# The values' chunk first in the second block, and loads released slot by slot

## The reference

```python
x = first_block(x, ...)    # mixer, then PEER: every token gathers 128 expert rows
x = second_block(x, ...)   # forgetting + band attention, layer norm, conv FFN, layer norm

# end of the first block: 8 heads x 16 experts a token, u and v rows of 1024 each
a = gelu(einsum('cd,chkd->chk', x_c, u_tab[e_c]))
x = x + gate2 * einsum('chk,chkd->cd', g_c * a, v_tab[e_c])
x = rmsnorm(x, norm_final_g)

# start of the second block
proj = x @ w_in            # q_a, k_a, v_a (512 columns each), forget gate (8), q_b, k_b, v_b
log_f = log_sigmoid(f_a + b_forget)
y_a = forgetting_attention(q_a, k_a, v_a, log_f)       # causal, decay from cumsum(log_f)
y_b = chunked_band_attention(q_b, k_b, v_b, rel_bias)
x = layer_norm(ALPHA * x + concat(y_a, y_b) @ w_out, ...)
```

## Time and profile before

| | |
|---|---|
| median of 3 runs | 1195.69 us |
| profiled execution | 1200.46 us, its span 1198.6 us |
| TensorE matmul busy | 1067.8 us, 89% |
| VectorE, ScalarE, GpSimd busy | 822.1, 427.7, 287.2 us |
| transfers | 389.39 MB, mean 325 GB/s |
| gathers (GpSimd's queue) | 268.45 MB, 54.2% of 16 engines' span |
| all other loads (SyncE's queue) | 120.07 MB, 25.6% |
| chain that ended last | TensorE 52%, DMA 30%, VectorE 12% |

### The profile page before, as it was taken

How to read it: one execution, slowest core, us unless ns; L and a number is a source line. 1 busy time by engine, 2 the same in 40 slices (tenths; PEclk the granted TensorE clock), 3 DMA queues, 4 the chain that set the end, 5 groups by cost and what they waited for, 6 DMA issues and landing times.

```text
span 1198.6 us, 13458 instructions
## 1 busy us (share of the span) xinstructions
PE 1067.8 (89%) x4938; PEld 711.9 (59%) x4938; DVE 822.1 (69%) x1893; ACT 427.7 (36%) x895; POOL 287.2 (24%) x260
## 2 busy tenths in 40 slices
PE   5998999999999987887877888778799999999997
PEld 3797986754444442332332333323399879999986
DVE  5697675757677677778887455555565677888843
ACT  3535631413332232222222111111365664656631
POOL 0000000345354442453544454444000000000000
PEclk8998999999999998888989899998889998999999
DMA  9984593999999999999999999999683342654530
GB/s 374 426 332 183 243 398 151 393 379 421 422 421 422 420 423 420 421 422 420 420 421 422 421 422 422 421 422 421 260 338 141 141 176 81 236 190 167 207 141 36
DMA packets 47878, 389.39 MB, mean 325 GB/s; under 512 B 5442, under 2 KB 5826, under 8 KB 7236
## 3 DMA queue, kind: packets, MB, share of 16 engines
q0 software_dynamic: 36864, 268.45, 54.2%
q1 hardware_dynamic: 10948, 120.07, 25.6%
HBM read 387.45 MB, written 1.05 MB: 324 GB/s over the span
## 4 chain that ended last, share of the span: by engine, by line
PE 52%; DMA 30%; DVE 12%; ACT 3%; issue 1%; POOL 1%; SPq 1%; DVEq 0%; POOLq 0%
DMA ring<-in_uv,idx 24%; PE ps L1783 17%; PE ps L1423 16%; PE ps L1909 5%; DMA ring<-in_w_ada 5%; DVE ring L1237 4%; PE ps L1634 2%; PE ps L1839 2%; PE ps L1445 2%; DMA ring<-in_w_in 2%; DVE ring L887 2%; PE ps L1581 1%; PE ps L1651 1%; DVE ring_r L876 1%; ACT L731 1%
## 5 line engine op out<-in xcount | busy, mean ns | idle before, releaser
L1783 PE MATMUL ps<-ring,probT 128*128 128x512 f32 x1020 | 500.6, 638 | 96.9 <-ACT probT L736 96.7
L1237 DVE CUSTOM_DVE_ANT_0 ring<-h2t,ring 128x1024 f32<-128x1024 f32 x255 | 308.8, 1223 | 169.1 <-DMA ring<-in_uv,idx 168.7
L1783 PEld LDWEIGHTS ps<-ring,probT 128*128 128x128 f32 x1020 | 201.4, 203 | 346.3 <-issue 205.8
L488 POOL DMA_INDIRECT ring<-in_uv,idx x255 | 286.0, 1121 | 346.0 <-PE ps L1783 288.8
L1423 PE MATMUL ps<-util_r,ring_r 128*128 128x256 f32 x1312 | 219.3, 285 | 0.5 <-DVE util_r L1209 0.5
L1423 PEld LDWEIGHTS ps<-util_r,ring_r 128*128 128x128 f32 x1312 | 183.9, 192 | 2.0 <-issue 1.9
L876 DVE TENSOR_TENSOR ring_r<-ring,ring_r 128x1024 fp32r<-128x1024 f32 x134 | 157.8, 1221 | 29.4 <-ACT ring_r L504 29.4
L504 ACT ACTIVATE ring_r<-ring 128x1024 fp32r<-128x1024 f32 x134 | 134.0, 1051 | 49.4 <-DMA ring<-in_w_in 25.8
L731 ACT ACTIVATE prob<-prob 128x2 f32<-128x2 f32 (+2 forms) x94 | 19.2, 204 | 367.5 <-DVE prob L1237 367.4
L1423 PE MATMUL ps<-h_r,ring_r 128*128 128x256 f32 x704 | 125.3, 281 | 0.0
L736 ACT ACTIVATE probT<-ct,prob 128x128 f32<-128x128 f32 x256 | 85.1, 392 | 73.8 <-DVE prob L1243 73.8
(11 more groups left out here) (214 smaller groups left out, 985.4 us busy)
## 6 DMA issues: line engine op xcount, KB each, us to landing
ring<-in_w_in SPq DMA_DIRECT2D x13, 2048.0 KB, 12.5
ring<-in_w_up SPq DMA_DIRECT2D x11, 2048.0 KB, 7.9
ring<-in_w_ada SPq DMA_DIRECT2D x7, 2048.0 KB, 9.8
ring<-in_w_down SPq DMA_DIRECT2D x6, 2048.0 KB, 7.9
ring<-in_w_ada SPq DMA_DIRECT2D x8, 1024.0 KB, 16.3
ring<-in_w_out SPq DMA_DIRECT2D x4, 2048.0 KB, 7.9
ring<-in_w_q SPq DMA_DIRECT2D x3, 2048.0 KB, 9.7
ring<-in_w_br SPq DMA_DIRECT2D x2, 2048.0 KB, 12.7
```

Of the source, the lines that this page charges most:

```text
L488: e.indirect_dma_start(out=row_buf[n], out_offset=None, in_=uv, in_offset=bass.IndirectOffsetOnAxis(ap=idx[:, tt, k:k + 1], axis=0)).then_inc(
L1237: e.tensor_tensor_reduce(u, h2t[:, tt, :], u, 1.0, 0.0, ALU.mult, ALU.add, av[:, tt, n % 128:n % 128 + 1]).then_inc(*made.put(("dot", n)))
L1783: ins = e.matmul(acc[half][:, :], diag[:, n % 8, :], row_buf[n][:, D + half * 512:D + (half + 1) * 512], start=(k == 0), stop=(k == 127))
```

## The change

Five edits that belong together.
1. `BATCHES`: steps 232 to 247 share a gelu by two, no longer by four.
2. The first chunk loaded and used in the second block is ("in2", 2), the values'. The first four go 2, 0, 1, 3 into slots 3, 0, 2, 1. Its quarters become Q2 to Q2+3, those of chunks 0 and 1 Q2+4 to Q2+11; `high_place` puts the quarters from Q2 on four places further, so that the first four lie in slot 5 (last step 248) and the next four in slot 4 (last step 255).
3. SyncE's wait for step 255's arrival is gone: each of the first four loads waits for the last step of its slot alone.
4. TensorE multiplies the values' first half for the first tile ahead of the second tile's turning, then the second half for the first tile, then both halves for the second tile, and only then the columns of chunks 0 and 1.
5. ScalarE and VectorE split Q2 and Q2+1 ahead of the last squares and sums, Q2+2 and Q2+3 ahead of the turned tile's split; the values are copied out of PSUM before the forget gate's work, the keys' second copy stands behind the lows of Q2+12 to Q2+15.

```diff
-    then = ([("in2", i) for i in range(6)] + [("out2", 0), ("out2", 1)]
+    then = ([("in2", i) for i in (2, 0, 1, 3, 4, 5)] + [("out2", 0), ("out2", 1)]
-    chunks = first + [(kind, i, slot) for (kind, i), slot in zip(then, [1, 0, 3, 2] * 6 + [1])]
+    chunks = first + [(kind, i, slot) for (kind, i), slot in zip(then, [3, 0, 2, 1] * 6 + [3])]
...
-Q2 = QUARTER["in2", 0, 0]
+Q2 = QUARTER["in2", 2, 0]
+def high_place(q):
+    return (q + (HI // 2 if q >= Q2 else 0)) % HI
-BATCHES = [(n, 2) for n in range(0, 96, 2)] + [(n, 4) for n in range(96, 248, 4)] + [(n, 1) for n in range(248, 256)]
+BATCHES = ([(n, 2) for n in range(0, 96, 2)] + [(n, 4) for n in range(96, 232, 4)] + [(n, 2) for n in range(232, 248, 2)]
+           + [(n, 1) for n in range(248, 256)])
...
-            sp.wait_ge(arrived[255], 255)
...
-                        act.wait_ge(done, ("rows", last_rows[NW + q % HI // 4]))
+                        act.wait_ge(done, ("rows", last_rows[NW + high_place(q) // 4]))
...
+            split_high(Q2, Q2 + 1)
             sqrt_table(45)
             row_squares(3, 1)
             row_root(3, 1)
-            split_high(Q2, Q2 + 1)
+            split_high(Q2 + 2, Q2 + 3)
             for half in range(2):
                 turned_high(3, hi_r, 1, half)
-            split_high(*range(Q2 + 2, Q2 + 8))
+            split_high(*range(Q2 + 4, Q2 + 10))
+            copy_unit(unit("in2", 0, 0), qa[:, 0:2, :], -0.125)
             act.wait_ge(made, "fe")
...
-            for z in (0, 2):
-                copy_unit(unit("in2", 0, z), qa[:, z:z + 2, :], -0.125)
-                split_high(Q2 + 8 + z, Q2 + 9 + z)
+            split_high(Q2 + 10, Q2 + 11)
+            copy_unit(unit("in2", 0, 2), qa[:, 2:4, :], -0.125)
             copy_unit(unit("in2", 1, 0), ka[:, 0:2, :])
             split_high(*range(Q2 + 12, Q2 + 16))
...
+            split_low(Q2, Q2 + 1)
             rows_added(3, 1)
             row_gain(1, 0)
             row_part(3, 1)
             row_gain(1, 1)
             row_diagonal(3, 1)
-            split_low(Q2)
+            split_low(Q2 + 2, Q2 + 3)
             for half in range(2):
                 turned_low(3, hi_r, lo_r, 1, half)
-            split_low(*range(Q2 + 1, Q2 + 4))
             x3_again(1)
             split_low(*range(Q2 + 4, Q2 + 8))
+            for tt in range(2):
+                dve.wait_ge(done, ("tokens", 2, tt))
+                e.tensor_copy(va[:, tt, :], bank(("tokens", 2, tt))[:, :]).then_inc(*made.put(("v", 2, tt)))
+            split_low(Q2 + 8, Q2 + 9)
...
-            split_low(*range(Q2 + 8, Q2 + 12))
+            split_low(Q2 + 10, Q2 + 11)
+            split_low(*range(Q2 + 12, Q2 + 16))
             copy_unit(unit("in2", 1, 2), ka[:, 2:4, :])
-            split_low(*range(Q2 + 12, Q2 + 16))
-            for tt in range(2):
-                dve.wait_ge(done, ("tokens", 2, tt))
-                e.tensor_copy(va[:, tt, :], bank(("tokens", 2, tt))[:, :]).then_inc(*made.put(("v", 2, tt)))
...
-            turned_x(3, 1)
-
             def both(k):
                 return [("x low", 3, 0, k // 4), ("x low", 3, 1, k // 4)]
 
+            tokens("in2", 2, 0, xs, lambda k: [("x low", 3, 0, k // 4)], (0,))
+            turned_x(3, 1)
+            tokens("in2", 2, 2, xs, lambda k: [], (0,))
+            for z in (0, 2):
+                tokens("in2", 2, z, xs, both, (1,))
             columns("in2", 0, 0, xs, both, acted)
...
             columns("in2", 1, 0, xs, both, acted)
             columns("in2", 1, 2, xs, both, made)
-            tokens("in2", 2, 0, xs, both)
-            tokens("in2", 2, 2, xs, both)
```

More of the change, by code:

```diff
@@ L65 @@
 USED = ("ada", "in", "br", "out", "keys", "q", "in2", "out2", "up", "down")
-QUARTERS = [(kind, i, slot, z) for kind, i, slot, nq in sorted(CHUNKS, key=lambda c: (USED.index(c[0]), c[1])) for z in range(nq)]
+QUARTERS = [(kind, i, slot, z) for kind, i, slot, nq in sorted(
+    CHUNKS, key=lambda c: (USED.index(c[0]), -1 if c[0:2] == ("in2", 2) else c[1])) for z in range(nq)]
 QUARTER = {(kind, i, z): q for q, (kind, i, _, z) in enumerate(QUARTERS)}
 SLOT_OF = {(kind, i): slot for kind, i, slot, _ in CHUNKS}
-Q2 = QUARTER["in2", 0, 0]
+Q2 = QUARTER["in2", 2, 0]
+def high_place(q):
+    return (q + (HI // 2 if q >= Q2 else 0)) % HI
 FIRST_BUFS = ((0, 1), (2, 0), (2, 1), (1, 0), (1, 1), (3, 0), (3, 1))
@@ L273, in quarter @@
             w, lo = part(slots[slot]), part(slots_r[slot])
-            a = NW * SLOT + (q % HI) * 1024
+            a = NW * SLOT + high_place(q) * 1024
             hi = ring_r[:, a:a + w.shape[1] * w.shape[2]].rearrange("p (k n) -> p k n", k=w.shape[1])
@@ L1426, in columns, with tokens @@
                 banks.give(name, freed, emptied or name)
-            def tokens(kind, i, z, x, x_ready):
+            def tokens(kind, i, z, x, x_ready, tiles=range(2)):
                 if z == 0:
-                    group(("tokens", i, 0))
-                    group(("tokens", i, 1))
+                    for tt in tiles:
+                        group(("tokens", i, tt))
                 q = QUARTER[kind, i, z]
-                a = NW * SLOT + (q % HI) * 1024
+                a = NW * SLOT + high_place(q) * 1024
                 wh = ring_r[:, a:a + 2048].rearrange("p (q k n) -> p k q n", q=2, k=KD)
```

## The result

The change made the kernel slower: median 1206.39 us against 1196.01 us, 9 runs each, ratio 1.0072 with a 95% interval of 1.0058 to 1.0087, that is 8.6 us (the two medians differ by 10.4 us; below, times are compared by the ratio and its interval, because the median of before itself moved between 1196.01 and 1199.62 us from one series of runs to the next). The prediction was 1209, slower, in a range of 1195 to 1215.

A forecast was written before the change was run, and what follows sets the result against it. Gathers bound the kernel until about 860 us, TensorE afterwards. With row 255 17.1 us late and gains of 2.35 and 1.6 us, S came 13.1 us later: 1195.7 + 13.1 = 1209 us, range 1195 to 1215.

The forecast's parts named there:

- Part 3: Second-block loads released by each slot's last row: alternating with gathers on the lagging engine, they make row 255 17.1 us late.
- the last dot: Start of the dot product of row 255, the last expert row: forecast at 876.4 us, 859.32 us before.
- the rows' end: Instant when TensorE finishes the expert rows: forecast 880.3 us, or 882.0 at half clock, against 865.55 before.
- S: Instant of the second block's first scores on TensorE, after which all was taken as fixed: forecast 924.5 us, 911.36 before.
- Row 255 is late by 3 x 4.9 + 4 x 0.61 = 17.1 us: On the lagging DMA engine, three whole loads and four packets of the fourth get in before the last row.
- its packets start about 1.3 us later: First early load, issued at 843.4 us: its packets start at 844.7 us, with rows 249 to 255 still queued.
- Part 2: Values' chunk first, behind the last rows: TensorE's waits removed, splits ahead of the row chain added; gain 1.6 us.
- Part 1: Late rows from 232 on in twos: TensorE's backlog goes, rows end at 863.2 us; gain 2.35 us, at worst 0.
- rival C: Other queue shares on the lagging engine: equal bytes 1205.3 us, loads first 1211.3, or 1214.3 with half clock; chance 0.20.
- A: Gathers keep their pace, or loads use only engines done early: S at 907.4, 1191.7 us, faster; chance 0.22.
- B: Loads get one packet per four to eight of the rows: row 255 late by 3.8 to 6.9 us; chance 0.12.
- D: Early release of loads doesn't happen because SyncE is held by another wait: about 1196 us; chance 0.01.

The follow-up runs named there:

- one_early: The changed kernel with only the first load let out behind step 246, the three others waiting for step 255's arrival: 1202.48 us, ratio 1.0039.
- half_early: The changed kernel with half the first chunk, in 8 KB packets, loaded behind step 246; all whole loads wait for step 255's arrival: one run, 1203.41 us.
- late_slots: The kernel before with steps 232 to 247 in twos, no wait for step 255's arrival, first loads into slots 2, 0, 3, 1: 1196.78 us, ratio 0.9991.
- twos: The kernel before with steps 232 to 247 in batches of two, nothing else changed: 1196.54 us, ratio 0.9989.
- nowait: The kernel before with only SyncE's wait for step 255's arrival removed: 1196.81 us, ratio 0.9995.

## Why the prediction was right, and where a size was off

**Part 3, direction and mechanism.** Right: the first load at 843.92 us (forecast 843.4), alternation packet by packet, 4.9 us a load on the path of the rows, no load wait behind the last row. The signs of the forecast came in part: the last dot at 869.34 us and not near 876, the rows' end at 873.48 and not near 881, S at 917.55 and not 925. The term that was mis-sized is "Row 255 is late by 3 x 4.9 + 4 x 0.61 = 17.1 us": it measured 9.8, two whole loads. The step under it that failed is "its packets start about 1.3 us later". With the row queue full the first packet came 3.5 us after the issue (847.4 us; also 3.4 in one_early, and 3.4 in half_early), against 1.0 us with empty queues in before and on the idle engines of late_slots. So row 250 landed untouched, its slot was free early, and the second load's packets stood right behind the first's; between them they held row 252 back by 8.6 us and row 253 by 9.8, which is what the working has for row 253. The term is lost at the third load: its packets were to start at 864.4 us. TensorE, at half clock behind 4.72 us of idle time (granted 0.50 over 862 to 866 us), had read row 252 only by 866.7 us, and the load was issued at 866.72. The idle engines took it up 1.0 us later, at 867.7; the one still busy with row 255 did not disturb it in the 2.6 us left to the last dot. So the third load (4.9 us) and the four packets of the fourth (2.4 us) cost nothing. The delay limits itself: each release waits for a row that the load before has delayed. That later start and later release are the cause is read from these instants; no run changed one of them alone, so how the 7.3 us divide between them is open.

The working also slips by its own rule: from 844.7 us to row 250's landing at 847.0 are seven packets of rows, so one for one the row would have been late by 4.3 us (seven of 0.61), not by 2.5. That lies in the part that the 3.5 us made void.

**Part 2.** S came 44.1 us after the end of the rows, forecast 44.2 (917.55 - 873.48). The gain set against it, 1.6 us, was off: before's 45.8 contains the whole turning at half clock (3.78 us) and a first load released late by the backlog (TensorE waits 0.51 us for the low part); twos, with a turning of 3.38 us and no such wait, has 44.4, so by these traces part 2 brings 0.3 us with weights at hand. The idle time it fills comes back as splits ahead of the row chain (2.4 us) and as the uncovered copy (1.0 us).

**Part 1.** Right in what it does, 2.35 us forecast, about 1.3 us measured (0.1 to 2.6), because the fall to half clock that it guards against is not in every execution. For the same reason the base was wrong: S of 911.36 us stood 3.5 us later than in an execution of the old order without the fall. The base's 3.5 us are 2.1 in the rows' end and 1.4 behind it, just what parts 1 and 2 were credited with removing. The errors had opposite signs: 7.3 us too much delay, 1.3 us too much gain in part 2 and 2.35 in part 1. So 13.1 was forecast; 13.1 - 7.3 + 1.3 + 2.35 is the 9.5 of the traces, and 8.6 was measured. That 1209 stands as near to the 1206.39 as it does is therefore in part luck: an error of 7.3 us was offset in part by two others, 3.65 us together. By the number alone the 1205.3 of equal bytes (rival C) fits as well; what decides is the traces.

**Rivals.** A (rows keep their pace) and B (a small share for loads) fall with the packet counts; equal bytes in C falls with the 1.84 MB against 0.79 in the same 6 us (half_early, where equal bytes and equal counts are the same, only shows that the bytes follow the size of the packets), loads first with the equal counts. D falls with the issue at 843.92 us, though nowait showed something near it: the wait by itself held next to nothing back. That fifteen engines finish early and one decides rests on the shares of the earlier trace rows; no run took that engine out of the path, so why it lags stays open.

## What to carry to other kernels

A transfer that is let out early is only free if every engine that it runs on has time to spare: count the packets that it puts in front of the last ones you wait for, and price them at their full time. Here that was 4.9 us for each load of 2 MB issued with rows queued, and nothing for loads issued 3.2 us ahead of the last dot. Moving work to the front of an in-order engine moves its wait there too, so an edit that relies on early data has to be judged together with the edit that makes the data early. And before a gain is set against a trace, look whether the stretch contains a fall of the clock that another execution doesn't have.

## What was not expected of the hardware

A load issued with seven gathers queued had its first packet after 3.4 to 3.5 us in three kernels, against 1.0 us with queues that were empty. In late_slots both stand side by side: idle engines took up the load after 1.0 us, and the one still at the rows not within 2.7 us. The Trainium skill states the turn by packets (DMA: Bandwidth & Descriptors, "Queues, rings and completion order"); the traces agree, 112 against 112 and 97 against 98 packets. That page calls 9 to 17 descriptors a typical packet; here, by the rhythm of 0.9 us and by row 251 being late by six packets of the load's eight, the turn changed after each one of 8 or 16 KB.

The same 2.8 us of idle time on TensorE, in the same place of the same order of work, was followed by the 1.2 GHz clock in one execution (before: granted 0.66 over 840 to 850 us) and not in another (nowait: 1.00 from 838 to 850 us).
